# Sliding-window attention moved in among the qkv projections, with twenty repeated native products, in a one-core encoder step

## The reference, cut to what matters

```python
def attn_qkv(h, pos, w_in, q_g, k_g):
    B, L, _ = h.shape
    q, k, v = jnp.split(h @ w_in, ODD_SPLITS, axis=-1)
    q = rope(rms_norm(q.reshape(B, L, C_HEADS, C_HDIM), q_g), pos)
    k = rope(rms_norm(k.reshape(B, L, C_KV_HEADS, C_HDIM), k_g), pos)
    return q, k, v.reshape(B, L, C_KV_HEADS, C_HDIM)
...
    s = jnp.einsum('bnqhgd,bnkhd->bnhgqk', qc, kw).astype(F32) * (C_HDIM ** -0.5)
    s = jnp.where(valid[None, :, None, None, None, :], s, -jnp.inf)
    p = sink_softmax(s, sinks)
    o = jnp.einsum('bnhgqk,bnkhd->bnqhgd', p.astype(v.dtype), vw)
```

## Time and profile before

| what | value |
|---|---|
| median of 3 runs | 1627.71 us (1624.07 to 1635.13) |
| profiled execution, own time | 1645.43 us |
| span of its instructions | 1643.7 us |
| mean granted clock of TensorE | 0.954 |
| PE busy | 1542.2 us, 94% |
| first to last qkv product | 599.4 to 661.9 us |
| first score product | 676.5 us |
| start of the `ao` projection | 746.1 us |

### The profile page before, as it was taken

The page is one execution under the profiler, slowest core; times in us unless marked ns, Lnnn a source line. Parts: engine busy times, 40 slices in busy tenths (PEclk is TensorE's granted clock), DMA queues, the critical chain, the costliest instruction groups (busy, mean ns, idle before and its releaser), DMA issues.

```text
span 1643.7 us, 22010 instructions
## 1 busy us (share of the span) xinstructions
PE 1542.2 (94%) x7901; PEld 1281.1 (78%) x7901; DVE 1076.4 (65%) x1032; ACT 879.8 (54%) x978; POOL 154.5 (9%) x163
## 2 busy tenths in 40 slices
PE   4998999899899999798899999999999999999996
PEld 3997556689899973568797888888888888888884
DVE  3666423554454424654547888888888889888884
ACT  3454103443333231533446777777777777777773
POOL 2012002120000012101014010000101000000100
PEclk8999999989899999658899999999999999999998
DMA  8342313259853451301049999999999999999991
GB/s 270 116 142 84 128 64 132 58 161 312 222 145 109 151 178 55 109 1 52 1 156 403 390 380 392 390 383 388 385 389 379 391 373 380 389 358 388 363 353 46
DMA packets 218432, 393.13 MB, mean 239 GB/s; under 512 B 11507, under 2 KB 84806, under 8 KB 218342
## 3 DMA queue, kind: packets, MB, share of 16 engines
q1 hardware_dynamic: 208646, 359.48, 61.0%
q0 software_dynamic: 9728, 32.91, 6.6%
HBM read 367.38 MB, written 26.28 MB: 239 GB/s over the span
## 4 chain that ended last, share of the span: by engine, by line
PE 54%; ACT 2%; issue 2%; DVE 1%; DMA 0%; DVEq 0%; POOL 0%; POOLq 0%; ACTq 0%
PE bank L1315 27%; PE bank L1333 13%; PE bank L898 4%; PE bank L1319 3%; PE bank L1241 2%; PE bank L1215 1%; PE bank L875 1%; PE bank L1343 1%; ACT part L1757 1%; PE bank L1284 1%; PE bank L1107 0%; DMA total<-view,view 0%; PE bank L1139 0%; PE bank L1145 0%; PE bank L1132 0%
## 5 line engine op out<-in xcount | busy, mean ns | idle before, releaser
L2374 DVE TENSOR_TENSOR part<-view,part 128x2048 fp32r<-128x2048 f32 x264 | 604.5, 2291 | 86.5 <-ACT part L1757 86.1
L1757 ACT ACTIVATE part<-view 128x2048 fp32r<-128x2048 f32 x264 | 506.4, 1918 | 133.4 <-PE bank L1315 84.0
L1315 PE MATMUL bank<-part,xg 128*128 128x512 f32 x1920 | 451.5, 392 | 1.2 <-DVE view L2449 1.2
L1315 PEld LDWEIGHTS bank<-part,xg 128*128 128x128 f32 x1920 | 359.1, 188 | 75.4 <-issue 1.3
L1333 PE MATMUL bank<-part,hidT 128*128 128x512 f32 x1056 | 248.0, 390 | 6.8 <-DVE hidT L2411 6.8
L1333 PEld LDWEIGHTS bank<-part,hidT 128*128 128x128 f32 x1056 | 197.6, 188 | 49.2 <-DVE part L2374 8.1
L1165 PE MATMUL bank<-hT,ffn_w 128*128 128x320 f32 x1056 | 163.5, 318 | 10.0 <-DVE ffn_w L2101 7.3
L1165 PEld LDWEIGHTS bank<-hT,ffn_w 128*128 128x128 f32 x1056 | 161.9, 196 | 11.4 <-issue 6.0
L898 PE MATMUL bank<-h,e_tile 128*128 128x320 f32 x576 | 90.6, 320 | 13.5 <-DVE h L1878 7.7
L898 PEld LDWEIGHTS bank<-h,e_tile 128*128 128x128 f32 x576 | 88.3, 196 | 15.6 <-issue 8.2
L2101 DVE TENSOR_TENSOR ffn_w<-view,ffn_w 128x2048 fp32r<-128x2048 f32 x22 | 50.4, 2292 | 50.1 <-ACT ffn_w L1635 50.1
(11 more groups left out here) (298 smaller groups left out, 1633.8 us busy)
## 6 DMA issues: line engine op xcount, KB each, us to landing
view<-in_moe_w SPq DMA_DIRECT2D x528, 512.0 KB, 9.2
view<-in_ffn_w SPq DMA_DIRECT2D x44, 512.0 KB, 5.9
slots<-view POOLq DMA_DIRECT2D x5, 2560.0 KB, 14.2
view<-in_even_w_in SPq DMA_DIRECT2D x6, 2048.0 KB, 15.2
view<-in_ffn_w SPq DMA_DIRECT2D x8, 1408.0 KB, 6.3
view<-in_attn_w_in SPq DMA_DIRECT2D x3, 2048.0 KB, 7.8
view<-in_xattn_w_k SPq DMA_DIRECT2D x2, 2048.0 KB, 10.0
view<-in_xattn_w_v SPq DMA_DIRECT2D x2, 2048.0 KB, 8.6
```

The costliest lines, as they stand in the source:

```text
L1315: ins = mm(H[g][w], xg[x][:, at], part[u % 3][r][:, (2 * c + w) * 512:(2 * c + w + 1) * 512], start=begin and n == 0, stop=done and n == 2)
L1757: A(part[u % 3][0], RAW[u % DEEP], ACT.Copy).then_inc(sg("split_hi"), 1)
L2374: V.tensor_tensor(part[u % 3][1], RAW[u % DEEP], part[u % 3][0].bitcast(F32), ALU.subtract).then_inc(sg("split_lo"), 1)
```

## The change

PE's order in the stage is rewritten. The groups 0 to 5 no longer wait for all turns: as soon as a block's heads are turned, scores, probabilities and values of the chunks that need only it are put between chunks of the later qkv products. Blocks 0 and 1 are turned inside `qkv(1, 2)` and `qkv(2, 2)`, groups 0 to 3 run wholly inside block 2's projections, and the scores of groups 4 and 5 too. Left behind the last projection are the probabilities and values of groups 4 to 7, the turns of block 2, and groups 8 and 9. Into that part go twenty products `keep_swa` (native float32, 128 rows, 320 columns, into bank 3, whose contents nobody reads after). The product with the last chunk of `qkv(2, 2)` stands after the scores of group 5.

Banks: qkv alternates between banks 0 and 1, the values of groups 0 to 3 use bank 3, later ones bank 2; probabilities use bank 2, then 0 and 1. The streams of ACT and DVE are rewritten to match: ACT's copies `qkv_rows`, `head_roots`, `turned_heads` and DVE's `head_squares`, `head_scale`, `head_turn` are now single steps between the steps of the groups. Blocks 0 and 2 share one `rot` row. The split of `ao` weight tiles 0 and 1 moves behind the copies of groups 8 and 9, and the wait for the outputs of POOL (`out_written`) moves there from group 0. `o2T` is four tensors in place of two.

PE's order after the change (the core of the diff):

```diff
+        def keep_swa(n):
+
+            for i in range(n):
+                mm(bank[3][:, 0:T], hT[:, 0, 0:P], hT[:, i, :], start=True, stop=True)
+
+        qkv_part(0, 0)
+        norm_by_token(3)
+        qkv_part(0, 1)
+        qkv_part(0, 2)
+        pe.wait_ge(sg("swa_cache_loaded"), 32)
+        transposes("cskT", [(kv * P, ckn[:, kv * 64:(kv + 1) * 64]) for kv in range(4)])
+        qkv_part(1, 0)
+        qkv_part(1, 1)
+        qkv_part(1, 2, range(0, 1))
+        turn_heads(0, range(0, 2))
+        qkv_part(1, 2, range(1, 3))
+        turn_heads(0, range(2, 4))
+        qkv_part(1, 2, range(3, 5))
+        turn_heads(0, range(4, 5))
+        qkv_part(1, 2, range(5, 8))
+        qkv_part(2, 0, range(0, 2))
+        read(pe, ("qkT", 0, 4))
+        scores(*GROUPS[0])
+        qkv_part(2, 0, range(2, 5))
+        scores(*GROUPS[1])
...
+        qkv_part(2, 2, range(0, 1))
+        probs(2)
+        qkv_part(2, 2, range(1, 2))
+        turn_heads(1, range(0, 2))
+        qkv_part(2, 2, range(2, 3))
+        values(2)
+        turn_heads(1, range(2, 4))
+        qkv_part(2, 2, range(3, 4))
+        turn_heads(1, range(4, 5))
+        probs(3)
+        qkv_part(2, 2, range(4, 5))
+        read(pe, ("qkT", 1, 4))
+        scores(*GROUPS[4])
+        qkv_part(2, 2, range(5, 6))
+        values(3)
+        qkv_part(2, 2, range(6, 7))
+        scores(*GROUPS[5])
+        qkv_part(2, 2, range(7, 8))
+        for i in range(4, 8):
+            probs(i)
+            if i < 6:
+                scores(*GROUPS[i + 2])
+            keep_swa(2)
+            values(i)
+        keep_swa(2)
+        turn_heads(2, range(0, 5))
+        keep_swa(2)
         read(pe, ("qkT", 2, 4))
-        scores(*GROUPS[0])
-        scores(*GROUPS[1])
-        for i, (c, g) in enumerate(GROUPS):
-            swa_tail(i, c, g)
+        scores(*GROUPS[8])
+        scores(*GROUPS[9])
+        keep_swa(4)
+        for i in (8, 9):
+            probs(i)
+            keep_swa(2)
+            values(i)
         read(pe, ("spv", 4, 1))
```

ACT's and DVE's orders from group 3 on:

```diff
+        swa_tail(3, *GROUPS[3])
+        exponentials(4)
+        window_high(*GROUPS[3])
+        exponentials(5)
+        qkv_rows(2, 2)
+        head_roots(2)
+        for i in range(4, 8):
+            swa_tail(i, *GROUPS[i])
+            if i < 6:
                 exponentials(i + 2)
-            if i < 2:
-                tile_high(AO + i)
+            window_high(*GROUPS[i])
+        turned_heads(2)
+        exponentials(8)
+        exponentials(9)
+        act.wait_ge(sg("out_written"), 16 * 11)
+        for i in (8, 9):
+            swa_tail(i, *GROUPS[i])
+            tile_high(AO + i - 8)
+            window_high(*GROUPS[i])
...
+        peaks(4)
+        window_low(3, *GROUPS[3])
+        peaks(5)
+        normalise(4)
+        head_squares(2)
+        swa_tail(4, *GROUPS[4])
+        normalise(5)
+        peaks(6)
+        head_scale(2)
+        window_low(4, *GROUPS[4])
+        swa_tail(5, *GROUPS[5])
+        peaks(7)
+        normalise(6)
+        head_turn(2)
+        window_low(5, *GROUPS[5])
+        swa_tail(6, *GROUPS[6])
+        normalise(7)
+        window_low(6, *GROUPS[6])
+        swa_tail(7, *GROUPS[7])
+        window_low(7, *GROUPS[7])
+        peaks(8)
+        peaks(9)
+        normalise(8)
+        normalise(9)
```

More of the change, by code:

```diff
@@ L237, in build @@
     qkv = split(take(3 * 1536), 3)
-    rot = split(take(3 * 1280), 3)
+    rot_rows = [take(1280) for _ in range(2)]
+    rot = [rot_rows[b % 2] for b in range(3)]
     rtmp = take(1280)
+    swa_at = top[0]
     top[0] = max(top[0], ARENA - (2 * 256 + 3 * 4 * 64 + 3 * 48))
@@ L1189, in _, with qkv_part, turn_heads @@
                         ins.then_inc(sg(f"w2_used{t}"), 1)
[L1191 to L1203, removed]
+        def qkv_part(b, u, chunks=range(KC)):
+            t0, n = BLOCKS[b]
+            key = ("qkv", b, u)
+            w = split(weights(pe, f"qkv{u}"), KC)
+            out = start(key) if 0 in chunks else bank[use[key][0]]
+            for k in chunks:
+                pe.wait_ge(sg("h_ready"), KC + k + 1)
+                ins = mm(out[0:n, :], hT[:, k, t0:t0 + n], w[:, k], start=k == 0, stop=k == KC - 1)
+            if KC - 1 in chunks:
+                end(ins, key)
+        def turn_heads(b, groups):
+            n = BLOCKS[b][1]
             pe.wait_ge(sg("rot_done"), 2 * b + 2)
-            for g in range(5):
-                transposes(("qkT", b, g), [(i * P, rot[0:n, b, (4 * g + i) * 64:(4 * g + i + 1) * 64]) for i in range(4)])
+            for g in groups:
+                transposes(("qkT", b, g), [(i * P, rot[b][0:n, (4 * g + i) * 64:(4 * g + i + 1) * 64]) for i in range(4)])
         def scores(c, g):
@@ L1225, in swa_tail, with values @@
                     transposes(("spT", c, g, k), [(j * P, sp_prob[i % 2][:, j, k * P:k * P + rows[k]]) for j in range(4)])
-            if i + 2 < len(GROUPS):
-                scores(*GROUPS[i + 2])
+        def values(i):
+            c, g = GROUPS[i]
+            rows = rows_of(c)
             for k in range(2):
@@ L1679, in _, with qkv_rows, head_roots @@
         norm_root_by_token(3)
[L1680 to L1684, removed]
+        def qkv_rows(b, u):
+            t0, n = BLOCKS[b]
+            key = ("qkv", b, u)
+            out = full(act, key)
+            A(qkv[0:n, b, u * 512:(u + 1) * 512], out[0:n], ACT.Copy, scale=rnat[0:n, b:b + 1]).then_inc(freed(key), 1)
+        def head_roots(b):
+            t0, n = BLOCKS[b]
             act.wait_ge(sg("qk_squares"), b + 1)
@@ L1687, in _, with turned_heads @@
             A(hstat[0:n, b, 0:20], hstat[0:n, b, 24:44], ACT.Exp, scale=-0.5).then_inc(sg("qk_rstd"), 1)
-        out = full(act, "cskT")
-        A(kTs[:, :, 0:P], split(out[0:64], 4), ACT.Copy).then_inc(freed("cskT"), 1)
-        for b, (t0, n) in enumerate(BLOCKS):
+        def turned_heads(b):
+            t0, n = BLOCKS[b]
             for g in range(5):
```

210 lines of the change are left out of this document (148 added, 62 removed).

## The result

The changed kernel takes 1624.95 us in the median of its twenty executions, the kernel before 1636.22. Without two disturbed executions of the changed kernel (2195 and 2198) its median is 1622.9 (1613 to 1633). The ratio of the two kernels is 0.9925, 95% interval 0.9900 to 0.9951: 12 us faster, 0.75%. In two later groups of runs, on two chips, the same pair gave 0.9939 (0.9917 to 0.9961) and 0.9942 (0.9912 to 0.9973). Carried to the 1627.71 of the prediction, the three are 1615.5, 1617.8 and 1618.3.

What follows compares the result with a forecast made beforehand. The stage lost about 8 us of PE idle and ran nearly all groups at half clock. `ao` 8.0 us earlier plus 2.0 at its start made 10.0 us: medians 1627.7 to about 1618, range 1608 to 1632.

Steps and rivals of the forecast that it cites:

- The woven part: First qkv product to last projection, local attention put among qkv chunks at full clock: 82.2 us, ending at 681.6.
- the rule quoted there: Changing the tiling mode drains TensorE; full drains around each piece (34 x 0.37 = 12.6 us) end this 10 us later.
- No wait within it: Among the qkv chunks no wait was charged: DVE and ACT have the time, head chains run under qkv products.
- The held weave: Rival: DVE and ACT queues hold PE within block 2's projections, each hold costing 4 to 8 us; 1622 to 1628, chance 0.08.
- The wait behind it: Behind the last projection PE waits for group 5's softmax steps and ACT's copy of `qkv(2, 2)`: 2.5 us (1.5 to 3.5).
- That wait lets the clock fall: The 2.5 us wait behind the last projection lets the clock fall to 0.50, as earlier waits did.
- Groups 4 and 5 at 0.50, clock back with group 6: Behind the wait: half clock for 28.0 us to 712.1 despite two products each, then full clock for 26.0 to 738.1.
- the clock holds: Rival: behind the last projection the clock never falls; `ao` at 729.1, 20 us gained, 1606 to 1613, chance 0.20.
- A product's price: Each added product behind the last projection costs 0.54 us at full, 1.08 at half clock, plus 0.15 to 0.2 a place.
- DVE's hold on group 6: If the clock holds, DVE's normalise 6 and head turn 2 delay the bank for group 6's values: about 3.5 us.
- The gain at `ao`: The first 5.9 us of `ao`, before at 0.50, run at full clock: 2.0 us saved (0 to 2.95).
- Slower: Rival: clock stays at 0.50 to the stage's end, twenty products at 1.08 on the path; 1640 to 1646, chance 0.07.

Runs made afterwards that it cites:

- the waits alone filled: Changed kernel with products only ahead of group 4's probabilities (four), group 8's (four) and `ao` (two), none within the groups: 1619.12 us, ratio 0.9877.
- both waits filled: Changed kernel with four more products ahead of group 4's probabilities and two ahead of `ao`: 1618.77 us, ratio 0.9877; run again 1620.02 us, 0.9922.

## Why the prediction was right, and where it wasn't

The time was right: 10 us forecast, 9 to 12 measured, in the range in all three groups of runs. The steps behind it were right up to 684 and wrong after it: the clock kept another course there, which the prediction itself names as a sign that the forecast is wrong.
- *The woven part.* Forecast 82.2 us from the first qkv product; measured 82.20 (later traces 81.7). The sum held; its terms were not timed one by one (the scores of groups 0 and 1, for one, took 1.10 each instead of 0.9). It also answers the rule quoted there: the Trainium skill, TensorEngine Tiling, Key Properties, by which this part would have ended 10 us later at the prediction's price of 0.37 us a change. No drain of that price shows in its length.
- *No wait within it.* 0.65 us idle in 82.2, of which 0.42 is a DMA wait behind the norm. The held weave is out.
- *The wait behind it.* Forecast 2.5, measured 2.01, ended by ACT's copy as named.
- *That wait lets the clock fall.* Right in all three traces, 0.4 to 2.0 us behind its end; filled, with the products of the groups in place, the clock stays to the end of the stage.
- *Groups 4 and 5 at 0.50, clock back with group 6.* This step failed. It said that two products each would not help, so 28.0 us at half clock. Measured: 3.4 to 7 us. The two products are what brings it back within group 4: without any the course is the forecast's, 0.51 to group 6, and with the waits alone filled groups 4 and 5 ran at 0.52. From the end of the wait to `ao` the step's sum was 54.0 us; 45.1 were measured. That is the 45.0 that I had worked out for the rival "the clock holds", by other terms: the clock was gone for 7 us, and DVE held group 6 for 0.74 instead of 3.5.
- *A product's price.* Two with their place 1.23 to 1.28 at full clock and about 2.4 at half; measured 1.24 to 1.34 and 2.50. Right.
- *DVE's hold on group 6.* Given as 3.5 us for the case that the clock holds; measured 1.84 when it did, 0.74 in the changed kernel.
- *The gain at `ao`.* 2.0 forecast (0 to 2.95); the half-speed stretch went from 5.9 us to 3.05, 1.4 us, or to none in the third trace.
- *Slower.* It would have needed 0.50 to the end; in the weave without products the last 20.7 us are just that (0.51), and even so that kernel, which has no products to pay for, isn't slower than before. With the products it didn't arise.

So why did the sum come out? In the traces the failed step is worth 9 us more than I gave. The medians don't show these 9 us, and the untraced executions of before include many at a better clock than the traced one that I worked from. I carried a difference from an execution 17.7 us above the median (of three runs; of twenty it is 9.2 above) to that median without asking whether a part of its slow stage was in the 17.7. If it was, two errors of like size met, and the sum was right by luck; that some 8 us of the stage of before are gone in its median execution is argued from the mean clock, not shown by a trace.

## What to carry to other kernels

Work that can't hold the clock should be put beside work that can, before anything is spent on idle products: in the woven order twenty products were worth some 5 to 7 us, in the old order nothing. Products belong first where PE waits. Inside groups 4 and 5 they were needed as well, and whether for the wait that they covered or for the groups' rows is open. Once the clock holds, look at once for the next engine's queue (3 us of DVE work out of the way gave 1.5). And before a difference from one trace is carried to a median, the traced run's place in the spread and its mean clock should be compared with those of the other runs.

## What the runs showed of the hardware

Small DVE operations took several times as long while GpSimd ran a tensor operation. With both waits filled, two that take 0.16 and 0.17 us took 1.01 and 0.65 between 682.6 and 684.3, while GpSimd's sine product ran from 681.26 to 684.28; a reduction out of PSUM in the same time took its usual 0.54. In the changed kernel one such small operation took 2.21 us at 644.81, beside the sine product of block 1. That GpSimd is the cause is read from these two places, not tested. And the granted clock differs from execution to execution in stretches whose instructions are the same (0.90 to 1.00 at 400 to 450 us): code that no one touched started the stage anywhere from 589.3 to 599.4 us.
